# A hybrid mixer and a grouped mixture of experts on one core: the mixer's last group is normed and routed tile by tile in the mixer's own block, the rounds are counted behind the tables, and the first expert's weights are loaded over the mixer's rows

## What is computed

```python
x = layer_norm(ALPHA * x + hybrid_mixer(x, w_in, ...) , ln_mix_g, ln_mix_b)      # called x1 below
probs = softmax(x @ router_w + router_b)                  # 16 experts per token
grp = argmax(sum of the two best probs in each of 4 groups)
top_p, top_local = top_k(probs of that group, 2)          # two experts per token
gates = top_p / top_p.sum(-1)
y = sum over the token's two experts e of gate * ((silu(x @ w_gate[e]) * (x @ w_up[e])) @ w_down[e])
out = layer_norm(ALPHA * x + y, ln_moe_g, ln_moe_b)
```

## Time and profile before

| | |
|---|---|
| median of 3 runs | 1700.78 us (1699.57 to 1702.06) |
| profiled execution: its own time | 1698.55 us |
| its span, first to last instruction | 1696.2 us |
| PE busy in the span | 1611.2 us (95%) |
| DVE, ACT, POOL busy | 1086.9, 659.3, 341.4 us |
| mean granted PE clock | 0.977 |

### The profile page before, as it was taken

How to read it: one execution, slowest core, us unless ns; L and a number is a source line. 1 busy time by engine, 2 the same in 40 slices (tenths; PEclk the granted TensorE clock), 3 DMA queues, 4 the chain that set the end, 5 groups by cost and what they waited for, 6 DMA issues and landing times. The chain is left out here.

```text
span 1696.2 us, 25177 instructions
## 1 busy us (share of the span) xinstructions
PE 1611.2 (95%) x9494; PEld 1395.9 (82%) x9494; DVE 1086.9 (64%) x1799; ACT 659.3 (39%) x919; POOL 341.4 (20%) x275
## 2 busy tenths in 40 slices
PE   7999999999999999999999279999999999999994
PEld 6888888888888888888888269999999999999993
DVE  3536867557676468665585756565676667666777
ACT  3224424143342343341433324443555455545551
POOL 1100015100052000250000012222333323233333
PEclk9999999999999999999999679999999999999997
DMA  7332336322434225253223626666777777777762
GB/s 238 125 100 75 125 125 215 92 91 92 157 138 162 75 75 184 93 197 100 75 100 125 260 68 206 205 208 202 230 243 244 223 234 251 249 228 234 245 210 95
DMA packets 118922, 279.48 MB, mean 165 GB/s; under 512 B 14688, under 2 KB 16864, under 8 KB 118288
## 3 DMA queue, kind: packets, MB, share of 16 engines
q1 hardware_dynamic: 91536, 188.68, 32.8%
q0 software_dynamic: 26688, 87.05, 17.3%
q10 hardware_dynamic: 576, 2.10, 0.3%
HBM read 232.80 MB, written 48.40 MB: 166 GB/s over the span
## 5 line engine op out<-in xcount | busy, mean ns | idle before, releaser
L1056 PE MATMUL mix_acc<-mix_xT_high,mix_w_high 128*128 128x512 f32 x640 | 256.2, 400 | 2.2 <-DVE mix_w_low L793 2.2
L793 DVE TENSOR_TENSOR mix_w_low<-mix_w_raw,mix_w_high 128x2048 fp32r<-128x2048 f32 x73 | 168.7, 2311 | 138.4 <-ACT mix_w_high L648 138.3
L1058 PE MATMUL mix_acc<-mix_xT_high,mix_w_low 128*128 128x512 f32 x640 | 250.7, 392 | 0.0
L1057 PE MATMUL mix_acc<-mix_xT_low,mix_w_high 128*128 128x512 f32 x640 | 249.9, 390 | 0.0
L648 ACT ACTIVATE mix_w_high<-mix_w_raw 128x2048 fp32r<-128x2048 f32 x73 | 139.8, 1915 | 237.8 <-PE mix_acc L1058 223.9
L1799 DVE TENSOR_TENSOR moe_gate_up_low<-kept_w_gate_up_raw,moe_gate_up_high 128x2048 fp32r<-128x2048 f32 x64 | 146.6, 2291 | 80.4 <-ACT moe_gate_up_high L1669 80.4
L2141 PE MATMUL moe_gate_psum<-moe_xT_high,moe_gate_up_high 128*128 128x288 f32 x512 | 154.1, 301 | 1.4 <-DVE moe_xT_low L1816 1.4
L2143 PE MATMUL moe_up_psum<-moe_xT_high,moe_gate_up_low 128*128 128x288 f32 x512 | 152.0, 297 | 0.0
L2142 PE MATMUL moe_gate_psum<-moe_xT_low,moe_gate_up_high 128*128 128x288 f32 x512 | 151.7, 296 | 0.0
L2142 PE MATMUL moe_up_psum<-moe_xT_low,moe_gate_up_high 128*128 128x288 f32 x512 | 151.6, 296 | 0.0
L2141 PE MATMUL moe_up_psum<-moe_xT_high,moe_gate_up_high 128*128 128x288 f32 x512 | 151.5, 296 | 0.0
(11 more groups left out here) (456 smaller groups left out, 3496.2 us busy)
## 6 DMA issues: line engine op xcount, KB each, us to landing
mix_w_raw<-in_w_in SPq DMA_DIRECT2D x57, 1024.0 KB, 5.3
kept_w_gate_up_raw<-in_w_gate SPq DMA_DIRECT2D x32, 1024.0 KB
kept_w_gate_up_raw<-in_w_up SPq DMA_DIRECT2D x32, 1024.0 KB
kept_w_down_raw<-in_w_down SPq DMA_DIRECT2D x32, 1024.0 KB, 8.6
mix_w_raw<-in_w_out SPq DMA_DIRECT2D x16, 1024.0 KB, 5.1
mix_x_rows<-in_x POOLq DMA_DIRECT2D x16, 512.0 KB, 4.6
kept_conv_or_residual<-in_x POOLq DMA_DIRECT2D x16, 512.0 KB, 5.4
x<-kept_conv_or_residual POOLq DMA_DIRECT2D x12, 512.0 KB, 3.3
```

Of the source, the lines that this page charges most:

```text
L793: dve.tensor_tensor(wl[:, stage % 2], raw[:, stage % 2], wh[:, stage % 2].bitcast(F32), ALU.subtract).then_inc(split_l, 1)
L1056: pe.matmul(out, ah, bh, start=first, stop=False)
L1057: pe.matmul(out, ah, bl, start=False, stop=False)
L1058: return pe.matmul(out, al, bh, start=False, stop=last)
```

## The change

1. The mixer's group 3 stands outside the loop as straight code. It leaves out the four `X` pieces, the weights of a further group and the rows of a further group.
2. In its stage 17 every tile is taken, combined and normed by itself. PE turns tile 0's rows between tiles 2 and 3. The rows are turned before the bias is added; the bias reaches the logits as `router_w` times `ln_b` (eight matmuls with one column in stage 6, added to the router's bias in `late_b`), for which SP loads `ln_b` once more as a column of 128 x 8 single numbers, among the constants at the start.
3. Routing of group 3 follows in the same block; `route` is gone, and with it one wait of all engines. The logits are made in two halves.
4. Expert 0's weights are loaded over the mixer's `xT` (gate and up) and q/k (down) as soon as the input projection is through, behind the last stage's weights in SP's queue.
5. `rounds_needed` stands in `experts` behind `tables`. The loop's count is 1 in a register, and each engine loads the real number at the end of the round.
6. `down` B writes the banks `pg[1]`, `pu[1]`. So B doesn't wait for A's taking; `gate_up` f = 1 of the next expert waits for B's taking instead.
7. ACT splits the first three gate/up pieces before the gathered rows come; POOL makes the three threshold rows (an iota and a cast each) among the constants at the start; group 0 makes the quarter offsets on DVE.

```diff
+            sp.dma_start(keep.bias_col[:], column(ln_b), allow_slow_non_contiguous=True).then_inc(consts_in, 16)
...
+                if not last:
+                    load_stage(g, 0, 1)
+            with sp.Fori(0, NG - 1) as g:
+                group(g, False)
+            group(NG - 1, True)
+            sp.wait_ge(acc_full, (NG - 1) * FULL + OUT0 * NT)
+            load_gate_up(sp, keep, w_gate[0], w_up[0])
+            sp.wait_ge(s1_ps, NG * NT)
+            sp.sem_inc(sp_idle, 1)
+            sp.wait_ge(num_ps, NG * NT)
+            load_down(sp, keep, w_down[0])
+            for t in range(NT):
+                sp.wait_ge(v.x1_ready, (NG - 1) * NT + t + 1)
+                row = (NG - 1) * GT + t * P
+                sp.dma_start(x1_dram[row:row + P], R[:, t]).then_inc(keep.late_x1, 16)
...
+                if last:
+                    for t in range(NT):
+                        one = slice(t, t + 1)
+                        act.wait_ge(lvar_done, g + t + 1)
+                        own.step(act.activation(lrs[:, one], lmv[:, one, 1], ACT.Ln, bias=eps[:, 0:1]))
+                        own.wait(g)
+                        own.step(act.activation(lrs[:, one], lrs[:, one], ACT.Exp, scale=-0.5))
+                        own.wait(g)
+                        if t == NT - 1:
+                            for half in range(2):
+                                turned_rows(act, v_last, g, 1, half)
+                        act.wait_ge(ln_gained, g * NT + t + 1)
+                        act.activation(R[:, t], R[:, t], ACT.Copy, scale=lrs[:, one]).then_inc(ln_done, 1)
+                        if t == NT - 2:
+                            for half in range(2):
+                                turned_rows(act, v_last, g, 0, half)
+                    logits_taken(act, v_last, g, 0, keep.late_b, False)
+                    turned_rows(act, v_last, g, NT - 1, 0)
+                    logits_taken(act, v_last, g, 1, keep.late_b, False)
+                    exponentials(act, v_last, g)
+                    act.wait_ge(split_l, NG * ST)
+                    for t in range(NT):
+                        act.wait_ge(v.x1_ready, g * NT + t + 1)
+                        act.activation(AX[:, t], R[:, t], ACT.Copy, scale=alpha).then_inc(ax_done, 1)
+                        act.wait_ge(ax_done, t + 1)
+                        row = g * GT + t * P
+                        act.dma_start(acc_dram[row:row + P], AX[:, t]).then_inc(keep.late_acc, 16)
+                    return
...
+                    if final and stage + 1 == ST:
+                        for t in range(NT):
+                            take(g, stage, range(t, t + 1))
+                            wait_apart(dve, dve_idle, *own.due(g))
+                            dve.bn_aggr(lmv[:, t], lstat[:, t]).then_inc(lvar_done, 1)
+                            dve.wait_ge(lvar_done, g + t + 1)
+                            dve.scalar_tensor_tensor(out=R[:, t], in0=R[:, t], scalar=lmv[:, t, 0:1], in1=lng[:],
+                                                     op0=ALU.subtract, op1=ALU.mult).then_inc(ln_gained, 1)
+                        def turned_half(t, half):
+                            dve.wait_ge(v.turned, g * NT + t + 1)
+                            dve.tensor_copy(v.x1T[t][:, 4 * half:4 * half + 4],
+                                            v.banks[t % 2][half][:].rearrange("p (c n) -> p c n", c=4))\
+                               .then_inc(late_taken, 1)
+                        def add_bias(t):
+                            dve.wait_ge(v.turned, g * NT + t + 1)
+                            dve.tensor_tensor(R[:, t], R[:, t], lnb[:], ALU.add).then_inc(v.x1_ready, 1)
+                        for half in range(2):
+                            turned_half(NT - 2, half)
+                        add_bias(0)
+                        turned_half(NT - 1, 1)
+                        add_bias(1)
+                        add_bias(2)
+                        centred_logits(dve, keep, v_last, own, g, g)
+                        add_bias(3)
+                        choices(dve, keep, v_last, own, g, g)
+                        ranks(dve, keep, v_last, own, g, g)
+                        return
...
-                        if (stage, t) in SLOT:
+                        if (stage, t) in SLOT and not (last and stage > LAST_Y):
                             extra(g, *SLOT[(stage, t)])
+                        if last and (stage, t) == (6, 0):
+                            for c in range(KC):
+                                ins = pe.matmul(aux[2][0:TW, 0:1], keep.router_w[:, c], keep.bias_col[:, c:c + 1],
+                                                start=(c == 0), stop=(c == KC - 1))
+                            ins.then_inc(bias_ps, 1)
+                        if last and (stage, t) == (7, NT - 1):
+                            pe.wait_ge(bias_taken, 1)
+                            pe.sem_inc(pe_idle, 1)
+                        if last and (stage, t) == (ST - 1, NT - 2):
+                            turn_rows(pe, keep, v_last, g, 0, R[:, 0], ln_done)
...
+            turn_rows(pe, keep, v_last, g, 1, R[:, 1], ln_done)
+            turn_rows(pe, keep, v_last, g, 2, R[:, 2], ln_done)
+            for taken in v.taken:
+                pe.wait_ge(taken, g * RT + 2)
+            logits(pe, keep, v_last, 0)
+            turn_rows(pe, keep, v_last, g, 3, R[:, 3], ln_done)
+            fold_logits(pe, keep, v_last, g, 0)
+            pe.wait_ge(late_taken, 3)
+            pe.wait_ge(v.taken[0], g * RT + 3)
+            logits(pe, keep, v_last, 1)
+            fold_logits(pe, keep, v_last, g, 1)
+            counts(pe, keep, v_last, g)
...
+        pb = (pg[1], pu[1])
...
-        def trips(engine):
-            return engine.value_load(keep.rounds[0:1, 0:1], min_val=1, max_val=keep.all_rounds)
+        def trips_wanted(engine, wanted, r):
+            wait_apart(engine, idle, rounds_known, r + 1)
+            engine.reg_mov(wanted, engine.value_load(keep.rounds[0:1, 0:1], min_val=1, max_val=keep.all_rounds))
+        def one_trip(engine):
+            wanted = engine.alloc_register("rounds_wanted")
+            engine.reg_mov(wanted, 1)
+            return wanted
...
-            n_rounds = trips(dve)
+            wanted = one_trip(dve)
             dve.wait_ge(keep.late_x1, RT * 16)
-            with dve.Fori(0, n_rounds) as r:
+            with dve.Fori(0, wanted) as r:
                 one_hots(r)
                 split_gu(r, 0)
                 tables(r)
+                rounds_needed(r)
...
+                if f == 1 and e:
+                    for done in (y_act, y_dve):
+                        pe.wait_ge(done, r * (2 * LAST) + 2 * e)
...
             def down(r, e, k):
-                if k == B:
+                if k == A and e:
                     for done in (y_act, y_dve):
-                        pe.wait_ge(done, r * (2 * LAST) + 2 * e + 1)
-                elif e:
-                    for done in (y_act, y_dve):
-                        pe.wait_ge(done, r * (2 * LAST) + 2 * e)
+                        pe.wait_ge(done, r * (2 * LAST) + 2 * e - 1)
                 for c in range(FC):
                     if k == A:
                         pe.wait_ge(hl_done, r * (NE * FC) + e * FC + c + 1)
@@ -2196,7 +2248,7 @@
                             pe.wait_ge(dn_l, r * (NE * 2) + 2 * e + c // 2 + 1)
                     for q in range(2):
                         s = slice(q * BANK, (q + 1) * BANK)
-                        ins = three(py[q][:], hTh[:, c, AT[k]], hTl[:, c, AT[k]], dh[:, c, s], dl[:, c, s],
+                        ins = three((py, pb)[k][q][:], hTh[:, c, AT[k]], hTl[:, c, AT[k]], dh[:, c, s], dl[:, c, s],
```

## The result

The changed kernel takes 1690.89 us (median of five runs, 1688.29 to 1691.68). Its ratio to the kernel before is 0.9944, 95% interval 0.9933 to 0.9955. It is faster by 9.9 us between the two medians, 12 us less than forecast, and lies outside the range.

The account below looks back on a forecast made before the run. PE is busy 95% of the span, with one hole between mixer and experts, mostly waiting for DVE. 1.5 - 2.0 - 15.9 + 0.25 - 6.5 + 0.6 = -22 us gives 1679 us, range 1674 to 1688.

Parts of the forecast that it names:

- Sum -2.0: Mixer's group 3: X pieces' transposes gone -3.6, bias matmuls +1.0, tile 0's turn +0.9, leaving the loop earlier -0.3 us.
- three signs of being wrong: First one-hot waiting for stores; PE idle in stage 15 or 16; PE waiting for ACT or DVE at f = 1.
- the upper bounds of the unknown costs: Start +0.8, bias matmuls 0.5, tail +3, end up to 1.5 us; said to make 1683 us at the top.
- The start.: Kernel start: the bias column's load ahead of stage 1's weights in SP's queue costs 1.5 us, 0.5 or 2.3 by two rows.
- Last tile to one-hots.: From DVE's last mixer tile to the first one-hot: 37.85 us before, 22.0 after, gain 15.9.
- "near 956": Sign of being right: one-hots begin some 16 us sooner, near 956 of the span, with no wait for DMA before them.
- The clock, feared to fall: PE's clock in the tail might fall to 1.2 GHz: tile 3's turn takes 1.8 us and the tail is 1.3 longer.
- The rival of the longer tail: Between mixer and one-hots: weights collide with residual rows or queues interleave worse, 4 to 9 us, 1683 to 1688; 13 in 100.
- The first expert.: Count between `tables` and `same` moves `same`'s end to 995.6, where gathered rows let PE turn at 995.4 before: +0.25 us.
- The experts and the end.: Experts: PE's waits for A go, -6.5 us; end: SP loads the count once more, +0.6, from nothing to 1.5.
- The rival in which the experts give it back: In the experts, B starts earlier and PE then waits for next weights or rows, losing the 6.5; 1685 us, 12 in 100.
- the slower one: In the experts, f = 1's wait for B, taken 9.2 us later, outweighs the gain; 1704 us and more, 3 in 100.

Follow-up runs that it names:

- its copy with the pad: Changed kernel with an unused 32-byte tile ahead of the X pieces, so they begin at a multiple of 64; 1678.9 us, ratio 0.9878.
- the kernel before with the same fault: Kernel before with unused 32-byte tiles around the X pieces, so they alone begin 32 bytes past a multiple of 64; 1712.38 us, ratio 1.0072.
- the late column: Changed kernel with the bias column's load issued ahead of the last group instead of among the start's constants; 1685.01 us, ratio 0.9915.
- the pair with matched X pieces: Changed kernel with X pieces at a multiple of 64, without and with the bias column loaded late; 1678.9 and 1676.12 us.
- the column alone: Kernel before with only the bias column's load added, where the change issues it, no other tile moved; 1702.95 us, ratio 1.0025.
- its copies without the column: Kernel before with 32-byte pads moving X pieces alone, all operands, or weights alone; 1712.38, 1699.05 and 1713.42 us.
- the four copies of the kernel before: Kernel before with X pieces, all operands or weights moved 32 bytes, or the column load added; 1712.38, 1699.05, 1713.42, 1702.95 us.
- the run that undid it: Changed kernel with X pieces at a multiple of 64 and late bias column, rounds counted ahead of the one-hots again; 1678.01 us, ratio 0.9876.
- the run with the old banks: Changed kernel with X pieces at a multiple of 64 and late bias column, B back in A's PSUM banks with old waits; 1680.82 us, ratio 0.9896.

## Why the prediction was wrong

**The step that failed** is a term that stands beside the one about group 3, "Sum -2.0", and was put at nothing without a reason: that all four groups' matmuls cost what they did. The change was read for what it moves in time, and the move of a tile in memory was taken as free. It cost 12 us: 12.0 by the medians (11.2 by the ratios) between the changed kernel and its copy with the pad, 12.8 in the kernel before with the same fault. No rival held it. The threshold rows on POOL and the quarter offsets were named and put at nothing, but the X pieces' new place was not named. None of the three signs of being wrong appeared either: all three look for waits, and this loss is none. With it repaired the kernel takes 1678.9 us, where 1679 was forecast. That it fits so closely is luck: the start cost more than was forecast, and beside its own runs of the kernel before the repaired one gains 20.7 us, not 22 (and the spans of the two profiles differ by 18.6). The working of group 3 itself was about right. From stage 1's first matmul to DVE's last taking the kernels with matched operands and the change take 896.97 to 898.84 us (1.7 to 3.5 less than the 900.51 before), the changed kernel 911.47. (A slip in the range changed nothing: the upper bounds of the unknown costs add up to 1684 us, not 1683.)

**The start.** Forecast +1.5, bounds 0.5 and 2.3; measured 2.8 to 4.9 us by three comparisons (the changed kernel against the late column 4.9 by the ratios, the pair with matched X pieces 2.8 and the column alone 4.5 by the medians). The mechanism was right, its size was not. The rows are, on SP and ACT, first before and then after:

```profile
22.16 12.56 SPq L530 DMA_DIRECT2D mix_w_raw<-in_w_in  x3
29.98 1.92 ACT L648 ACTIVATE mix_w_high<-mix_w_raw 128x2048 fp32r<-128x2048 f32 x1 [13.89 <-DMA mix_w_raw<-in_w_in]
```

```profile
13.47 1.42 SPq L557 DMA_DIRECT2D kept_ln_bias_column<-in_ln_mix_b  x1
...
23.42 0.96 SPq L548 DMA_DIRECT2D mix_w_raw<-in_w_in  x2
33.10 1.91 ACT L684 ACTIVATE mix_w_high<-mix_w_raw 128x2048 fp32r<-128x2048 f32 x1 [17.52 <-DMA mix_w_raw<-in_w_in]
```

The load took 1.42 us of SP's time, and the weights behind it were issued 1.26 us later. But they also landed later: from that issue to ACT's split it took 9.7 us in place of 7.8. The working counted the issue and left out the queue behind it. How much of the later landing is the column's doing and how much the spread of the start from one execution to the next isn't shown: among the four profiles of the kernel before and its copies without the column, stage 1 started earliest, by 1.1 us, in that of before. PE's clock came on top: between 30 and 45 us it was granted 0.77 after and 0.89 before, as the last two windows of the start above show, so part of the stage then ran at the lower level, 1.2 GHz. The Trainium skill ("DMA: Bandwidth & Descriptors", Rules for kernel authors) says that a non-contiguous last dimension lowers to one descriptor per element. The 2.3 that the prediction took for that case was nearer than its 1.5, and also too low.

**Last tile to one-hots.** Forecast 22.0 us, measured 20.9 after and 20.9 in the copy with the pad; "near 956" for the one-hots would be right but for the 14 us that the mixer lost ahead of it. The steps: a DVE turn of 3.1 for a tile (945.91 to 948.97: 3.06), choices from 11.2 to 20.8 behind the last taking (10.7 to 20.2). The stores of x1 landed in 2.7 us each instead of 18.8, and nobody waited for them. The clock, feared to fall before the turn of tile 3, had not yet: it was granted 1.00 until 958 us, and that turn took 1.09 us, not 1.8.

```profile
953.90 1.09 PE L160 MATMUL mix_aux<-kept_identity,kept_conv_or_residual 128*128 128x128 f32 x8
```

The rival of the longer tail didn't come about.

**The first expert.** Forecast +0.25, measured +1.4. `same` begins 23.87 us behind the first one-hot step (969.86 to 993.73) where the working gives 22.6 (18.66 before, by the earlier trace rows, and 3.9 for the count). PE's table matmuls between them took 10.04 us instead of 9.12, which is most of that difference. But this part scatters: from one-hots to the experts' first matmul the four copies of the kernel before take 29.49, 29.51, 30.25 and 30.33 us where before took 28.94, so that most of the +1.4 can be chance. The count's place was worth 3.4 to 3.9 us by the trace of the run that undid it.

**The experts and the end.** Forecast -6.5 and +0.6, measured -5.0 together. The run with the old banks gives the first as 5.2 to 6.0 us by the traces, 8.4 against the one profile at 686.8, and 6.3 to 6.8 us by the ratios, with its wait of 6.1 as forecast. Its 695.2 against the 694.5 to 694.9 of the kernel before and its copies leaves 0.2 to 0.7 for the end, which agrees with the 0.6, but so few executions don't prove it. No wait at f = 1 appeared. The rival in which the experts give it back, and the slower one, are refuted.

## What to carry to other kernels

When PE is full and its busy time grows while its work shrinks, compare the median of one kind of matmul between the two profiles before looking for waits: 5 ns a matmul shows in no list of waits, and was 12 us here. A change that moves a tile to another pool or side must say at which byte it begins, and where the two operands of a matmul begin should be compared. The same place modulo 64 bytes was not enough in the experts' `down`; the same place modulo 256 is what all the 389 ns matmuls of the mixer share. A load that is small in bytes but made of single numbers is to be costed by what stands behind it in its queue, in landing as well as in issue, and belongs behind the first thing that the busiest engine waits for.

## What the runs showed of the hardware

A matmul of the mixer (split, fp32r operands, 512 columns) takes 389 ns by the median when both of its operands begin at the same place modulo 64 bytes (both at 0 in the kernel before, both 32 past in the run with all operands moved), and 394 to 396 ns when one begins 32 past and the other doesn't, whichever of the two it is. In `down` of the experts a shift of 64 bytes between the operands cost 4.4 to 4.7 ns in the mean, in the one run that had it. With 288 columns a shift of 32 cost 0.8 to 2.5 ns. The period is thus longer than 64 bytes; the experts' chunks speak for 256, which no run tested, nor do the runs say why it is so. The transposes of the mixer, in float32 and with 128 columns, don't show it: those of `x_rows`, 32 past a multiple of 64 beside an identity at one, take 272 ns in the mean before and after, as do those of the rows routed in the loop before, whose operands both begin at multiples of 128.
